# A two-layer hybrid attention decoder on one core: the scores of the next pair of heads wait for an earlier step of VectorE

## The reference

```python
def masked_softmax(s, mask):
    s = jnp.where(mask, s, NEG_BIG)
    m = jnp.max(s, axis=-1, keepdims=True)
    p = jnp.where(mask, jnp.exp(s - m), 0.0)
    return p / jnp.maximum(jnp.sum(p, axis=-1, keepdims=True), 1e-30)
...
o = g[..., 0:1] * o_c + g[..., 1:2] * o_s + g[..., 2:3] * o_w
```

## Time and profile before

| | us |
|---|---|
| median of 3 runs | 1416.3 |
| lowest and highest run | 1408.98 and 1417.31 |
| the profiled execution's own time | 1414.1 |
| its span, first to last instruction | 1412.4 |
| the stage of `prompt1` within the span | 917 to 1008 |

### The profile page before, as it was taken

The page is one execution under the profiler, slowest core; times in us unless marked ns, Lnnn a source line. Parts: engine busy times, 40 slices in busy tenths (PEclk is TensorE's granted clock), DMA queues, the critical chain, the costliest instruction groups (busy, mean ns, idle before and its releaser), DMA issues.

```text
span 1412.4 us, 26283 instructions
## 1 busy us (share of the span) xinstructions
PE 1283.0 (91%) x10100; PEld 1031.2 (73%) x10100; DVE 779.2 (55%) x1632; ACT 341.8 (24%) x897; POOL 243.7 (17%) x327
## 2 busy tenths in 40 slices
PE   7997798958998889999999999977788799999996
PEld 4454576737887788899999945655445468999996
DVE  1804645574567571576785457468343217767742
ACT  2124534433432231100000011457433301000000
POOL 1103000052422331111120110330022111111100
PEclk9998799979999999999999999979799799999999
DMA  7437697886547570454435442430147653544350
GB/s 275 152 109 268 204 334 271 279 284 230 179 152 241 196 237 12 132 167 153 146 124 166 162 153 88 147 99 1 42 159 222 221 179 121 178 142 139 124 164 34
DMA packets 150783, 236.12 MB, mean 167 GB/s; under 512 B 10594, under 2 KB 113250, under 8 KB 150242
## 3 DMA queue, kind: packets, MB, share of 16 engines
q1 hardware_dynamic: 138290, 201.91, 43.1%
q0 software_dynamic: 8208, 30.44, 6.4%
q10 hardware_dynamic: 4160, 2.10, 0.5%
HBM read 229.09 MB, written 13.64 MB: 172 GB/s over the span
## 4 chain that ended last, share of the span: by engine, by line
PE 80%; DVE 6%; DMA 4%; SPq 3%; issue 3%; ACT 3%; POOL 0%; POOLq 0%; DVEq 0%; ACTq 0%
PE ps L756 19%; PE ps L547 11%; PE ps L781 11%; PE ps L512 10%; PE ps L847 7%; PE ps L722 5%; PE ps L652 2%; PE ps L734 2%; DMA ring<-in_cache_kv 2%; SPq L394 2%; PE ps L978 2%; SPq L504 2%; PE ps L553 1%; PE ps L704 1%; DMA ring<-in_state_win 1%
## 5 line engine op out<-in xcount | busy, mean ns | idle before, releaser
L512 PE MATMUL ps<-ct,ring 128*128 128x128 f32 x960 | 146.4, 293 | 29.7 <-issue 9.6
L847 PE MATMUL ps<-big,proj 128*128 128x168 f32 (+1 forms) x1024 | 161.8, 311 | 3.6 <-DVE big L1790 3.6
L512 PEld LDWEIGHTS ps<-ct,ring 128*128 128x128 f32 x960 | 113.6, 148 | 69.6 <-issue 46.1
L547 PE MATMUL ps<-ring,xT 128*128 128x512 f32 (+1 forms) x384 | 160.6, 574 | 0.6 <-DMA ring<-in_w_in 0.6
L847 PEld LDWEIGHTS ps<-big,proj 128*128 128x128 f32 x1024 | 150.6, 193 | 8.5 <-issue 8.0
L547 PEld LDWEIGHTS ps<-ring,xT 128*128 128x128 f32 x384 | 70.0, 192 | 78.9 <-issue 77.2
L756 PE MATMUL ps<-kT,proj 128*128 128x144 f32 x960 | 124.1, 286 | 0.0
L756 PEld LDWEIGHTS ps<-kT,proj 128*128 128x128 f32 x960 | 120.3, 190 | 0.0
L1109 ACT ACTIVATE big<-ps 128x512 f32<-128x512 f32 (+3 forms) x172 | 87.3, 532 | 114.1 <-PE ps L512 113.6
L2050 POOL TENSOR_TENSOR big<-rows 128x576 f32<-128x576 f32 x22 | 51.0, 2317 | 261.4 <-DVE rows L1686 228.1
L756 PE MATMUL ps<-xT,ring 128*128 128x144 f32 x640 | 84.9, 286 | 0.0
(11 more groups left out here) (296 smaller groups left out, 2101.7 us busy)
## 6 DMA issues: line engine op xcount, KB each, us to landing
ring<-in_cache_kv SPq DMA_DIRECT2D x128, 512.0 KB, 5.7
ring<-in_w_gu SPq DMA_DIRECT2D x44, 1024.0 KB, 7.7
ring<-in_w_in SPq DMA_DIRECT2D x11, 2048.0 KB, 8.0
ring<-in_w_down SPq DMA_DIRECT2D x16, 1408.0 KB, 6.5
ring<-in_cache_kv SPq DMA_DIRECT2D x128, 128.0 KB, 3.2
ring<-in_cache_kv POOLq DMA_DIRECT2D x128, 128.0 KB, 3.5
ring<-in_w_out SPq DMA_DIRECT2D x4, 2048.0 KB, 9.8
ring<-in_state_win SPq DMA_DIRECT2D x16, 512.0 KB, 5.3
```

The lines of the kernel that those rows point to most:

```text
L512: return nc.tensor.transpose(out, in_, C("ident", 0, rows, rows))
L547: last = mm(ps[b + t][:, 0:w], xT[:, k, t * P:(t + 1) * P], src[:, k, :], start=k == 0, stop=k == KD - 1)
L847: last = mm(cmp_out(u, si, n), w1s(s, o)[:, hf * P:(hf + 1) * P], XS[(4 * kp + si) % XB][:, o, 0:n], start=o == 0, stop=o == 7)
```

## The change

The third addition of `first(h)` now counts on `a_m[1]`, and DVE waits for it there and no longer by `link`. Each head thus adds two to `a_m[1]`: one at the end of its additions, one at the end of L1868. PE waits for the additions of head 2j-1 ahead of scores(j), where it waited for that head's L1868. ACT waits for L1868 as before, by the new count.

```diff
             def prompt1():
                 def scores(j):
                     if j >= 1:
-                        pe.wait_ge(a_m[1], 2 * j)
+                        pe.wait_ge(a_m[1], 4 * j - 1)
...
             def prompt1():
                 def probs(h):
-                    act.wait_ge(a_m[1], h + 1)
+                    act.wait_ge(a_m[1], 2 * h + 2)
...
                     tt(W[:, 0:384], A[:, 0:384], C("causal"), ALU.add)
                     tt(W[:, 384:768], B[:, 0:384], C("causal"), ALU.add)
-                    link(tt(W[:, 768:798], A[:, 384:414], C("cmpcausal"), ALU.add))
+                    tt(W[:, 768:798], A[:, 384:414], C("cmpcausal"), ALU.add).then_inc(a_m[1], 1)
+                    dve.wait_ge(a_m[1], 2 * h + 1)
                     for x, lo, hi, step in parts:
                         last = v.reduce_max(st[:, b + lo:b + hi:step], x, AX)
                     link(last)
```

## The result

The changed kernel took 1401.52 us (median of 4 runs, 1401.02 to 1402.25) where the kernel before took 1416.8 (4 runs, 1408.98 to 1417.43): ratio 0.9901, 95% interval 0.9876 to 0.9926. Timed again beside more runs of both, it was 1403.86 (7 runs, 1396.12 to 1407.67) against 1415.67 (29 runs): 0.9914, interval 0.9881 to 0.9947. The change gained 12 to 15 us, about 1%, where 5.2 us were forecast.

The account below looks back on a forecast made before the run. The prediction saw no engine full in the prompt attention stage, with PE, DVE and ACT handing pairs round. Releases of 1.34, 1.03, 1.89 and 0.99 summed to 5.2 us, clock unchanged: 1410 us, range 1403 to 1417.5.

Parts of the forecast that it names:

- What bounds the stage: Second layer's prompt attention, 917 to 1008 us: no engine full; PE, DVE and ACT hand one pair of heads round.
- The size of one release: Scores can begin after DVE's third addition, beside the maxima, instead of after the last small step: 1.34 us earlier.
- The sum, 5.25: Prompt attention stage: 1.34 + 1.03 + 1.89 + 0.99 us from pairs 1, 2, 4 with 5, and 7.
- Its parts by pair: Gains by pair: 1.34 us in pair 1, 1.03 in 2, 1.89 in 4 and 5 together, 0.99 in 7.
- Pairs 3 and 6, put at nothing: Pair 3's scores idle only 0.26 us and DVE enters head 6 without a wait; pair 6 repeats it: no gain.
- the terms 1.03, 1.89 and the last 0.99: Pair 2 limited by PE's transposes, pairs 4 and 5 together, and pair 7 held by ACT's copy of head 11.
- Carried through behind the stage: Decode stage follows the last output copy and its transfer moves with PE, so the whole 5.2 us reaches the end.
- The clock: PE's granted clock in the stage taken as unchanged, size nothing; +3.45 us a pair and -2.8 kept for the range.
- case (a): Clock holds through pair 5, or falls where it costs nothing: 5.2 + 2.8 = 8.0 us gained; chance 0.19.
- (b): Clock falls for one pair more in the stage: 5.2 - 3.45 = 1.8 us gained; chance 0.15.
- (c): Clock low in two pairs more, among pairs 3 to 6: 1.7 us lost; chance 0.07.
- (d): Release has no effect, as PE's transposes or the next wait eat each gain: time as before; chance 0.07.

Follow-up runs that it names:

- e11: Kernel before the change, with unread matmuls filling PE's idle time at the start, ahead of later pairs' scores and in the tail: 1407.26 us, ratio 0.9927.
- e10: Changed kernel with unread matmuls ahead of pair 1's scores, between the first transposes and in the tail: 1396.51 us, ratio 0.9845.
- e1: Changed kernel with the new semaphore counts, but scores of every pair waiting for the last small step again: 1417.06 us, ratio 1.0006.
- e9: Kernel before the change, with unread matmuls on PE ahead of the scores of pairs 3 to 7 only: 1413.9 us, ratio 0.9966.
- e2: Changed kernel with the early release of the scores kept in pairs 1 and 2 only: 1410.3 us, ratio 0.997.
- e3: Changed kernel with the early release of the scores kept in pairs 3 to 7 only: 1409.49 us, ratio 0.9957.
- e7: Changed kernel timed again without an edit, beside more runs of the kernel before: 1403.86 us, ratio 0.9914.
- e4: Kernel before the change, with unread matmuls on PE ahead of the scores of pairs 1 to 7 and in the tail: 1403.24 us, ratio 0.9924.
- e6: Changed kernel with each head's scores written by themselves and released by the additions of the head two before: 1417.88 us, ratio 1.0022.

## Why the prediction was wrong

**What bounds the stage, and the release: right.** The size of one release, 1.34 us, is what pair 1 gained (4.98 to 3.64 of idle time on PE, and 1.34 between e11 and e10). Nothing of it was paid for: the maxima stayed at 1.10, and no cost of the counts is to be seen (e1). The sum, 5.25, was measured as 4.94 with the clock up in both kernels.

**Its parts by pair: one right, the sum near by luck.** Between e11 and e10, the release of pair 1 gives the forecast 1.34. Pair 2 gives 0.40 in place of 1.03, pairs 4 and 5 together 1.31 in place of 1.89, pair 7 with all behind it 0.57 in place of 0.99. Pairs 3 and 6, put at nothing, give 0.65 each. In the kernel before their scores waited only 0.26 and 0.27 us, behind a pair at the lower clock; with the clock up throughout (e11) these pairs take 8.30 us like the others. So a row without a wait there belonged to the clock, not to the pair. For pair 4 the prediction had two gains, 0.55 on DVE and 0.99 on PE's line, and let the larger one count; the runs put it at 0.65, where DVE is full. The errors nearly cancel, and no run shows the terms 1.03, 1.89 and the last 0.99.

**Carried through behind the stage: not contradicted.** The decode stage did not give the gain back. That it got 2.0 us shorter itself cannot be put down to the change, as the table below shows.

**The clock: the step that failed.** It is the sentence "I take the clock as it was". The term stood at nothing. Here are the length in us and the clock of the same stretches in seven profiles, six without filling and e9, whose pairs 0 to 2 and tail are not filled either:

| profile | pairs 0 to 2 | pairs 3 to 6 | pair 7 to the end | decode stage |
|---|---|---|---|---|
| before | 30.03, 0.66 | 36.49, 0.91 | 23.21, 0.75 | 127.94, 0.88 |
| e1, waits as before | 30.06, 0.66 | 36.49, 0.91 | 23.21, 0.75 | 128.00, 0.89 |
| e2, release in pairs 1, 2 | 23.73, 0.78 | 37.38, 0.86 | 20.44, 0.92 | 125.95, 0.91 |
| e9, before, loop filled | 26.65, 0.74 | 34.85, 0.95 | 24.12, 0.70 | 125.85, 0.92 |
| e3, release in pairs 3 to 7 | 25.63, 0.73 | 30.69, 1.00 | 21.98, 0.84 | 123.73, 0.91 |
| after | 27.13, 0.69 | 30.72, 1.00 | 20.79, 0.92 | 125.94, 0.91 |
| e7, after again | 22.79, 0.78 | 30.69, 1.00 | 22.59, 0.82 | 125.81, 0.89 |

One column goes with the change every time: in pairs 3 to 6 the clock fell in all three profiles without release and filling there (before, e1, e2) and stayed at 1.00 in all three with the release (e3, after, e7). These pairs got 5.8 us shorter, 2.6 by the release (four times 0.65) and 3.2 by the clock. e4 shows the same share without any release: 36.49 to 33.20. The prediction named it as case (a), priced it at 2.8, which is near, and gave it 0.19. With it the gain is 4.94 + 3.2 = 8.1 us, the 8.0 of case (a).

The medians gained 4 to 7 us more, and where these come from stays open. Between the profiles of before and after 2.42 us lie from pair 7 on and 2.00 in the decode stage, but neither goes with the release: e2, without the release of pair 7, has the shorter tail, e7 with it one of 22.59, and e11, whose decode stage begins at a clock of 1.00, has the longest of all:

```profile
984.97:1005.41 20.44, 13.99 (x116) 9.26 (x116) 10.36 (x34) 14.24 (x60) 0.00 (x0) 0.92 0.00 1
```

```profile
998.74:1127.23 128.49, 103.19 (x696) 60.97 (x696) 43.36 (x128) 41.94 (x96) 27.95 (x52) 0.89 0.55 178
```

The clock of the whole span is higher in the runs of the changed kernel (0.956 against 0.950), so the rest is likely a matter of the clock too; in which stretch, and why, one profile a kernel does not tell. The prediction looked at pair 5 alone. PE's tail ran at the lower level in part as well (0.75), and filled, at 1.00, it took 18.84 us in e4 in place of 23.21: of that the prediction had no term.

**Its direction.** The prediction said that the rows do not tell whether the clock holds, from two pairs with like idle times. What it had for case (a), the same work in less time, was borne out. The loop before had PE idle ahead of the scores for 0.96 to 1.27 us (pairs 4, 5 and 7) and ahead of the second transposes for 1.3; after, 0.31 ahead of the values and 1.3. e9 is the exception that shows the limit of this: there the clock fell at the scores of pair 3, behind 0.73 us of idle time, and the loop stayed at 1.00 only from pair 4 on. What exactly the chip measures was not tried.

The Trainium skill, "TensorE: Matmul & The Clock Gate", section "A second HAM failure mode: psum-queue depth-cycling", has it of another kernel that short idles between groups of matmuls make the clock swing. The traces here agree in both directions: the clock stood at 0.82 in pairs 5 and 6 before and at 1.00 after, and filling the idles of the kernel before brought the stage from 0.79 to 1.00 (e11). The prediction quoted it and then let two pairs outweigh it.

**The rivals.** (a) came, and more than it; (b), (c) and (d) did not: the clock fell in no pair more, and the release acted in every pair. The lower end of the range was drawn from the lowest run of before less about 6, not from what the clock could give in start and tail; it ended 1.5 us above the first median and 0.9 below the second.

## What to carry to other kernels

In a stage in which TensorE works in short groups with idle time between, look at the granted clock first: here filling alone was worth 13.0 and 14.2 us of the stage's 89.7 in the profiles of e4 and e11, and 11.1 and 8.5 us in their medians; the moved wait was worth 4.9 of the stage. An edit that closes gaps of TensorE should be priced twice, for the wait and for the stretches of its loop that stood at the lower clock. A pair without a wait next to a pair at the lower clock is no proof that the wait is harmless there. And where the clock differs between executions, a gain that one profile shows in a stretch is compared with the same stretch in profiles that leave it alone, before it is put down to the change.

## What the runs showed of the hardware

Matmuls that nobody reads, put into idle time of TensorE, made a kernel faster: e4, with some 70 instructions more, by 11.1 us in the median and 13.0 in the stage; e10's stage is 5.4 to 8.0 us shorter than the two of the changed kernel (76.07 and 78.64 to 70.63).

The order in which the same 24 matmuls of a pair are issued matters: they took 1.93 us with the two halves of the partitions taking turns and 3.28 with one half at a time (e6), at the same clock of 1.00. The order of the banks differed with it.
